# Norm statistics per token in 128x5 blocks, a router fed from raw rows, modulation of gathered rows

## The reference, cut to what is touched

```python
def rms_norm(x, g):
    y = x * lax.rsqrt(jnp.mean(x * x, axis=-1, keepdims=True) + EPS)
    return y * g

def layer_norm(x, g, b):                    # over 512 channels, in the convolution branch
    mu = jnp.mean(x, axis=-1, keepdims=True)
    var = jnp.mean(jnp.square(x - mu), axis=-1, keepdims=True)
    return (x - mu) * lax.rsqrt(var + EPS) * g + b

h = rms_norm(x, lp['rms1_g']) * (1 + sc1) + sh1
...
x = x + g1 * ((ga * y_a + gb * y_b + gc * y_c) @ lp['w_out'])
h2 = rms_norm(x, lp['rms2_g']) * (1 + sc2) + sh2
x = x + g2 * expert_choice_ffn(h2, lp['w_router'], lp['w1'], lp['w3'], lp['w2'])

# expert_choice_ffn, cap = 2 * L // 16: 64 latent and 16 context rows for an expert
aff = jax.nn.softmax(jnp.einsum('bld,de->ble', h, w_router), axis=-1)
gate, idx = lax.top_k(jnp.swapaxes(aff, 1, 2), cap)
xs = jax.vmap(lambda hb, ib: hb[ib])(h, idx)
hid = silu(einsum(xs, w1)) * einsum(xs, w3)
ye = einsum(hid, w2) * gate[..., None]
```

## Time and profile before

| | before |
|---|---|
| time, median of 3 runs | 3113.67 us (3109.89 to 3114.95) |
| profiled execution | 3115.0 us, its span 3113.2 us |
| mean granted clock of TensorE | 0.962 |
| PE busy | 2849.4 us (92%) |
| DVE busy | 1902.1 us (61%) |
| ACT busy | 1502.8 us (48%) |
| DMA read and written | 595.30 MB, mean 191 GB/s |

### The profile page before, as it was taken

One profiled execution on the slowest core, in us unless ns is written; L12 is line 12 of the kernel. 1 busy time (PEld: TensorE's weight loads), 2 busy tenths in 40 slices (PEclk: granted clock), 3 DMA queues, 4 the chain that ended last, 5 costly groups with the idle time before them and its releaser, 6 DMA issues.

```text
span 3113.2 us, 40542 instructions
## 1 busy us (share of the span) xinstructions
PE 2849.4 (92%) x16600; PEld 2226.8 (72%) x16600; DVE 1902.1 (61%) x1901; ACT 1502.8 (48%) x1939; POOL 345.1 (11%) x221
## 2 busy tenths in 40 slices
PE   7999998999996999999779999889999779999996
PEld 6888886888874666666478877778888546666664
DVE  3266556643337888888633666658233488888884
ACT  4244545112226777777532455441122267777773
POOL 0411100000001121111113011100000011111110
PEclk9999998999998999999989999999999889999998
...
GB/s 235 55 102 74 87 89 62 75 68 55 113 204 235 367 376 373 375 375 373 295 53 68 75 102 102 64 63 68 72 55 111 115 283 373 375 374 371 373 375 189
DMA packets 373481, 595.30 MB, mean 191 GB/s; under 512 B 12976, under 2 KB 164656, under 8 KB 373040
## 3 DMA queue, kind: packets, MB, share of 16 engines
...
...
## 4 chain that ended last, share of the span: by engine, by line
PE 68%; DMA 14%; DVE 8%; ACT 5%; issue 3%; SPq 1%; POOL 0%; DVEq 0%; POOLq 0%; ACTq 0%
PE ps L1188 17%; PE ps L1190 16%; PE ps L1189 16%; DMA m_raw<-in_w 11%; PE ps L1425 9%; PE ps L1350 2%; DVE m_lo L1125 2%; PE ps L1383 2%; DMA raw<-in_w_ada 1%; PE ps L1234 1%; ACT probs L513 1%; PE ps L1263 1%; DVE stats L971 1%; PE ps L1372 1%; DMA raw<-in_w_in 1%
## 5 line engine op out<-in xcount | busy, mean ns | idle before, releaser
L779 ACT CAST m_hi<-m_raw 128x2048 fp32r<-128x2048 f32 x384 | 732.9, 1911 | 319.5 <-DMA m_raw<-in_w 271.4
L1125 DVE TENSOR_TENSOR m_lo<-m_raw,m_hi 128x2048 fp32r<-128x2048 f32 x384 | 861.3, 2284 | 16.6 <-PE ps L1190 9.9
L1188 PE MATMUL ps<-h_hi,w_hi 128*128 128x320 f32 (+2 forms) x1408 | 444.6, 316 | 38.1 <-DVE h_lo L896 19.6
L1189 PE MATMUL ps<-h_lo,w_hi 128*128 128x320 f32 (+2 forms) x1408 | 438.7, 312 | 0.0
L1190 PE MATMUL ps<-h_hi,w_lo 128*128 128x320 f32 (+2 forms) x1408 | 438.7, 312 | 0.0
L1188 PE MATMUL ps<-m_hi,xs_hi 128*80 128x512 f32 x1024 | 405.8, 396 | 8.6 <-DVE xs_lo L1142 8.6
L1190 PE MATMUL ps<-m_hi,xs_lo 128*80 128x512 f32 x1024 | 403.3, 394 | 0.0
L1189 PE MATMUL ps<-m_lo,xs_hi 128*80 128x512 f32 x1024 | 403.3, 394 | 0.0
L851 DVE TENSOR_TENSOR w_lo<-raw,w_hi 128x2048 fp32r<-128x2048 f32 x68 | 157.9, 2322 | 303.8 <-ACT w_hi L556 293.5
L556 ACT CAST w_hi<-raw 128x2048 fp32r<-128x2048 f32 x46 | 87.5, 1904 | 528.7 <-DMA raw<-in_w_gate 354.1
L1188 PEld LDWEIGHTS ps<-h_hi,w_hi 128*128 128x128 f32 x1408 | 269.3, 191 | 44.1 <-issue 43.6
...
## 6 DMA issues: line engine op xcount, KB each, us to landing
m_raw<-in_w SPq DMA_DIRECT2D x384, 1024.0 KB, 10.3
...
```

The costliest lines, as they stand in the source:

```text
L779: nc.scalar.copy(m_hi[:, g % HIS], m_raw[:, g % RAWS]).then_inc(s["m_high"], 1)
L1125: nc.vector.tensor_tensor(m_lo[:, g % LOS], m_raw[:, g % RAWS], m_hi[:, g % HIS].bitcast(F32), ALU.subtract).then_inc(s["msplit"], 1)
L1188: pe.matmul(out, wh, xh, start=first, stop=False, skip_group_check=True)
L1189: pe.matmul(out, wh, xl, start=False, stop=False, skip_group_check=True)
```

## The change

All norm statistics are made per token instead of for every partition. A block of 128 tokens becomes the stationary operand and one column of ones the moving one, so that the sums of five blocks stand in five PSUM columns, 128x5 (`square_sums`): 40 matmuls of one column instead of 16 of 320, and 20 instead of 8 for each of the two LayerNorm sums. Root and reciprocal work on 128x5 (`row_scale`). Where the features need them as rows, `spread` multiplies each column, broadcast to 128x128, with the identity (5 matmuls of 128 columns) into PSUM, and DVE reads its factors from there. In norm 1 `spread` stands right behind the sums on PE, in layer 0 ahead of `ada_ahead`; in the merge it stands behind the first branch product of steps 6 and 7 and waits for the statistics.

Norm 2 isn't applied to all rows. The router gets raw x: its columns are scaled by `coef` once (`rv`, two DVE operations), its shift is made by 16 matmuls behind output chunk 0 (`rt_bias`, with a modulation column broadcast as the stationary block and 16 moving columns). `row_stats(c)` makes ten square sums of one column and ten logits products of 16 columns for the two feature chunks of output chunk c; it stands behind output chunk c+1, and the last one at the end. DVE scales the logits by the tokens' factor and adds the shift. The norm's multiplications, its sixteen modulations, the copy `cum` and its transposes go. `h_rows` gets x times the tokens' factor (ACT), and `coef` and shift are applied to the gathered rows of each expert, after their transposes (`rows_modulated`: two DVE operations on 128x640, with the factors laid out for the slots once in a layer by `slot_modulation`, four copies behind L1118). For that `turn_rows` moves from n=9 to n=8, `rows_high` from n=9 to n=10, `rows_low` from n=10 to n=11. ACT's first casts wait for `h_rows` instead of `routed`. The next layer's modulation products move behind the transposes to rows. The output projection cuts its columns 384 and 256 instead of 320 and 320, and the last transposes have three PSUM buffers instead of four. The diff, cut (ACT, DVE and PE in the order of the file):

```diff
+                act.wait_ge(s["r_ready"], seen("r_ready", 2))
                 for t in range(TT):
                     act.wait_ge(s["h2tok_ps"], seen("h2tok_ps"))
                     b = 2 * (t % 2)
-                    nc.scalar.copy(t_all[:, t], flat[:, b * 512:b * 512 + D]).then_inc(s["h2tok"], 1)
+                    nc.scalar.mul(t_all[:, t], flat[:, b * 512:b * 512 + D], st[:, 28 + t:29 + t]).then_inc(s["h2tok"], 1)
...
-                act.wait_ge(s["routed"], seen("routed"))
+                act.wait_ge(s["h2_out"], seen("h2_out", 16 * TT))
...
+            def row_scale():
+                dve.wait_ge(s["ss"], seen("ss"))
+                nc.vector.tensor_scalar(st[:, 28:33], ps[:, 6, 0:TT], 1.0 / D, EPS, ALU.mult, ALU.add).then_inc(s["row_a"], 1)
+                dve.wait_ge(s["row_b"], seen("row_b"))
+                nc.vector.reciprocal(st[:, 28:33], st[:, 28:33]).then_inc(s["r_ready"], 1)
+                dve.wait_ge(s["r_ready"], seen("r_ready"))
...
+                row_scale()
+                dve.wait_ge(s["r_spread"], seen("r_spread"))
                 for k in range(KT):
-                    nc.vector.tensor_tensor(mm_[:, k], x[:, k], row[:], ALU.mult).then_inc(s["tnorm"], 1)
+                    nc.vector.tensor_tensor(mm_[:, k], x[:, k], flat[:, 6 * 512:6 * 512 + TOK], ALU.mult).then_inc(s["tnorm"], 1)
...
+                coefficients(l, 32, "rms2")
+                router = small_at("router").rearrange("p (k e) -> p k e", e=EXPERTS)
+                dve.wait_ge(s["mods_ready"], 2 * l + 2)
+                for c in range(2):
+                    ins = nc.vector.tensor_tensor(rv[:, :, c, :], router, coef[:, :, c:c + 1].to_broadcast([P, KT, EXPERTS]), ALU.mult)
+                ins.then_inc(s["rt_w"], 1)
...
-                coefficients(l, 32, "rms2")
-                norm()
+                row_scale()
 
                 dve.wait_ge(s["logits"], seen("logits"))
-                nc.vector.tensor_copy(cum[:].rearrange("p (a n) -> p a n", a=2), ps[0:EXPERTS, 4:6, 0:HALF]).then_inc(s["logits_out"], 1)
-                dve.wait_ge(s["logits_t"], seen("logits_t"))
                 lg = ps[:, 7, 0:TT * EXPERTS].rearrange("p (t e) -> p t e", e=EXPERTS)
-                link(nc.vector.tensor_reduce(st[:, 8:13], lg, AX.X, ALU.max))
-                nc.vector.tensor_tensor(aff[:], lg, st[:, 8:13].unsqueeze(2).to_broadcast([P, TT, EXPERTS]), ALU.subtract).then_inc(s["rt_a"], 1)
+                link(nc.vector.tensor_tensor(aff[:], lg, st[:, 28:33].unsqueeze(2).to_broadcast([P, TT, EXPERTS]), ALU.mult))
+                nc.vector.tensor_tensor(aff[:, 0:4], aff[:, 0:4], rb[:, 1:2, :].to_broadcast([P, 4, EXPERTS]), ALU.add)
+                link(nc.vector.tensor_tensor(aff[:, 4], aff[:, 4], rb[:, 0], ALU.add))
+                link(nc.vector.tensor_reduce(st[:, 8:13], aff[:], AX.X, ALU.max))
...
+                def slot_modulation():
+
+                    for tile, of in ((coef_t, coef), (shift_t, mods_of[l][:, 24:24 + KT])):
+                        nc.vector.tensor_copy(tile[:, :, 0:CAP_LAT], of[:, :, 1:2].to_broadcast([P, KT, CAP_LAT]))
+                        ins = nc.vector.tensor_copy(tile[:, :, CAP_LAT:], of[:, :, 0:1].to_broadcast([P, KT, CAP_CTX]))
+                    link(ins)
+
+                def rows_modulated():
+
+                    dve.wait_ge(s["xs_ps"], seen("xs_ps"))
+                    link(nc.vector.tensor_tensor(xsm[:], ps[:, 2:4, :].rearrange("p b (k n) -> p (b k) n", k=4)[:, :, 0:SLOTS], coef_t[:], ALU.mult))
+                    nc.vector.tensor_tensor(xsm[:], xsm[:], shift_t[:], ALU.add).then_inc(s["xs_mod"], 1)
...
                     low(g)
+                    if g == 0:
+                        rows_modulated()
                 rows_low()
...
                             turned_low(1)
-                        if n == 10 and e < EXPERTS - 1:
+                            if e < EXPERTS - 1:
+                                rows_modulated()
+                        if n == 11 and e < EXPERTS - 1:
...
+            def square_sums(k0, k1):
+
+                for k in range(k0, k1):
+                    pe.wait_ge(s["sq"], seen("sq"))
+                    for t in range(TT):
+                        ins = pe.matmul(ps[:, 6, t:t + 1], mm_[:, k, t * P:(t + 1) * P], ones[:, 0:1], start=((k, t) == (0, 0)),
+                                        stop=(k == KT - 1), skip_group_check=True)
+                return ins
+
+            def spread(t_sem, t_count, sem):
+
+                pe.wait_ge(s[t_sem], t_count)
+                for t in range(TT):
+                    ins = pe.matmul(flat[:, 6 * 512 + t * P:6 * 512 + (t + 1) * P], st[:, 28 + t:29 + t].to_broadcast([P, P]), ident[:], start=True, stop=True)
+                ins.then_inc(s[sem], 1)
...
-                sum_squares(KT, "sq")
+                square_sums(0, KT).then_inc(s["ss"], 1)
+                spread("r_ready", 2 * l + 1, "r_spread")
                 if l == 0:
-                    ada_ahead((4, 5, 6, 7), (ada_in_a, ada_in_b))
-                    ada_turned(0, 2)
+                    ada_ahead((2, 3, 4, 5), (ada_in_a, ada_in_b))
...
-                            pe.matmul(ps[:, 6, :], ones[:], zc[:, j, 0:LAT], start=(j == 0), stop=(j == GROUPS - 1), skip_group_check=True)
-                            ins = pe.matmul(ps[:, 7, 0:CTX], ones[:], zc[:, j, LAT + CPAD:CRUN], start=(j == 0), stop=(j == GROUPS - 1), skip_group_check=True)
+                            for t in range(TT):
+                                at = t * P if t < 4 else LAT + CPAD
+                                ins = pe.matmul(ps[:, 6, t:t + 1], zc[:, j, at:at + P], ones[:, 0:1], start=((j, t) == (0, 0)),
+                                                stop=(j == GROUPS - 1), skip_group_check=True)
...
+                        if i in (LN_MEAN, LN_VAR) and n == 0:
+                            spread("ln_stat", seen("ln_stat"), "ln_spread")
...
+                def row_stats(c):
+
+                    pe.wait_ge(s["xo_done"], seen("xo_done"))
+                    ins = square_sums(2 * c, 2 * c + 2)
+                    if c == 3:
+                        ins.then_inc(s["ss"], 1)
+                    if c == 0:
+                        pe.wait_ge(s["rt_w"], seen("rt_w", 0))
+                    for k in (2 * c, 2 * c + 1):
+                        for t in range(TT):
+                            ins = pe.matmul(ps[:, 7, t * EXPERTS:(t + 1) * EXPERTS], x[:, k, t * P:(t + 1) * P], rv[:, k, 1 if t < 4 else 0, :],
+                                            start=((k, t) == (0, 0)), stop=(k == KT - 1), skip_group_check=True)
+                    if c == 3:
+                        ins.then_inc(s["logits"], 1)
...
                     if c == 0:
-                        feature_by_k(u, u, "mg_low")
+                        pe.wait_ge(s["rt_w"], seen("rt_w"))
+                        for n in range(2):
+                            for k in range(KT):
+                                ins = pe.matmul(ps[:, 6, (n + 1) * EXPERTS:(n + 2) * EXPERTS], mods_of[l][:, 24 + k, n:n + 1].to_broadcast([P, P]),
+                                                small_at("router")[:, k * EXPERTS:(k + 1) * EXPERTS], start=((n, k) == (0, 0)), stop=(k == KT - 1),
+                                                skip_group_check=True)
+                        ins.then_inc(s["rt_bias"], 1)
                     else:
-                        feature_split(u, u, halves)
+                        row_stats(c - 1)
...
+                pe.wait_ge(s["h2tok"], seen("h2tok", 2))
                 if l < DEPTH - 1:
+                    ada_ahead((4, 7, 2, 3), (ada_in_a, ada_in_c))
                     ada_turned(l + 1, 4)
...
-                        if n == 9 and e < EXPERTS - 1:
-                            turn_rows()
+                            if e < EXPERTS - 1:
+                                turn_rows()
```

160 lines of the change are left out of this document (77 added, 83 removed).

## The result

The changed kernel takes 3155.36 us, median of 4 runs (3154.69 to 3156.08). The kernel before took 3113.14 beside it. The ratio is 1.0137 with a 95% interval of 1.0119 to 1.0154: 42 us slower. The forecast was 3149.9, range 3120 to 3172. The profiled execution took 3156.08 us, span 3154.3, 41.1 over the span of before.

What follows compares the result with a forecast made beforehand. TensorE was taken as the bound outside the experts, the weight stream inside them. Terms 8.7+13.9+2.6+0.6+6.0+1.0+3.4 = +36.2 us on the median of 3113.67 gave 3149.9 us, range 3120 to 3172.

Steps and rivals of the forecast that it cites:

- (1): Start of layer 0: slower square sums, then statistics and spread ahead of the modulation products, +8.7 us.
- (2): Four LayerNorm sums: twenty sparse matmuls each plus spread instead of dense sums, +3.5 us each, +13.9 in all.
- second rival: Clock falls only in streams of 40 in a row, bursts of 16 or 20 keep it: 3130 us, chance 0.09.
- (3): Output projection to first MAX8: added PE matmuls against a shorter tail, +2.6 us in layer 0, +0.6 in layer 1.
- E: End of the last output-projection product; the forecast put the first MAX8 at E+19.5 us.
- (4): Top-k to the first expert product: a longer DVE sequence up to xs_lo, +3.0 us in each layer.
- (5): Steady experts: DVE's chain 1.2 us late at a border, delay paid once, +1 us for both layers.
- third rival: PE stalls at every expert because DVE's 7.4 us chain doesn't move forward: about 3190 us, chance 0.08.
- (6): Layer 0 to layer 1: slower sums, shorter statistics and spread, slower products behind, +3.4 us.
- (7): Next layer's modulation moved behind the token transposes, and three PSUM buffers instead of four: put at nothing.
- first rival: The clock holds in sparse streams, making the kernel faster: 3103 us, chance 0.11.
- attention (0): Projections and attention, up to the first gate cast: no change forecast, 0 us.

Runs made afterwards that it cites:

- experiment 6: Changed kernel with norm 1 and LayerNorm sums 128 columns wide, row sums and logits 96 wide, xs_hi and xs_lo casts one step earlier: 3111.31 us.
- experiment 1: Changed kernel with 128 moving columns of ones instead of one in the sums of norm 1 and the LayerNorm: 3140.81 us.
- experiment 2: Changed kernel with the cast of xs_hi at n=9 instead of 10 and xs_lo at n=10 instead of 11: 3146.97 us.
- 8: Kernel before with two extra DVE operations per expert at n=9 and xs_lo at n=11 instead of n=10: 3130.33 us.
- 5: Kernel before with two extra DVE operations per expert at n=9, written to an unread tile, xs_lo unmoved: 3116.95 us.
- 4: Kernel before with two extra DVE operations per expert at n=2, written to an unread tile: 3115.82 us.
- (9): Kernel before with two extra DVE operations per expert at n=9 and the gathered rows turned at n=8 instead of n=9: 3127.34 us.

## Why the prediction was right, and where it was not

The time and the direction held, and the mechanism given for the direction is there: the clock falls in or behind the streams of few columns. Between the traces of the changed kernel and of experiment 6 (40 us), the four stretches whose sums were widened (start, merge, output projection, layer 0 to 1) make up 35 us and the experts 17; attention and top-k went 12 the other way. But that the sum came within 6 us is luck. One term was too small by 25.7 us, one too large by 11, and 10 us in attention, put at nothing, are chance as far as the traces go. The largest term of the measured sum, the experts, is one that the prediction put at 1. It would have made the kernel slower with the clock held too: the 3111 us of experiment 6 and its 17 us less in the experts give some 3128, an estimate.

(1) *Start of layer 0*, +8.7: measured 9.1. The forty sums cost 16.04 us, not 14.5. From the start of the sums the first product is 10.1 us later than before in the changed kernel and 0.9 in experiment 1: all but about 1 us is the clock.

(2) *LayerNorm*, +3.5 each: measured 7.6 a layer, 3.8 each. The split was another one. In layer 0 the sums kept their clock nearly to their end (4.9 and 4.4 us instead of 5.9), and the dense products behind them lost it (3.0 and 1.8 us, against experiment 1, instead of the 0.8 put there). These bursts are paid for mostly after they have ended. The test named in the prediction, a clock of 0.50 over the LayerNorm sums and over the row sums between the output chunks, would have gone against it: the mean is 0.90 and 1.00 over layer 0's LayerNorm sums, and over the row sums and logits between the chunks it is 0.71 at 890.17 and 1.00 at 911.94. By that sign it was the second rival, in which bursts keep their clock; but its +5.2 for both layers, against 15.2 measured, left out the products behind them.

(3) *Output projection and top-k*, +2.6 and +0.6: measured −1.4 and −6.8. MAX8 came at E+17.0 in both layers, not E+19.5: the row sums and logits of chunk 2 ran wholly at the full clock (4.4, not 5.9), and so did a part of those of chunk 3. The additions between the chunks came to 16.9 and 13.5 us, not 18.4. The step that failed is the fall put at 3.0 us after the start of every burst: it came in the changed kernel between 1 and 5 us after it. Nor is E+17.0 fixed. Experiment 1 has these forty matmuls as they are, and there the fall came 2.3 us behind E, with MAX8 at E+20.2 in both layers:

```profile
917.86 2.29 PE L1307 MATMUL ps<-ones,m 128*128 128x1 f32 x20
920.01 4.29 PE L1558 MATMUL ps<-router_scaled,x 128*128 128x16 f32 x20
924.14 4.41 PE L1307 MATMUL ps<-ones,m 128*128 128x1 f32 x20
928.40 4.43 PE L1558 MATMUL ps<-router_scaled,x 128*128 128x16 f32 x20
```

(4) +3.0 a layer: measured 2.5. The copies for the slots took 1.0 us, not 2.1; DVE waited 2.6 us for the turned rows, about as reckoned.

(5) *Steady experts*, "the delay is paid once", +1: measured 26.7. This step failed. The arithmetic was right: 7.4 us of chain, 1.2 us late. Wrong was the sentence that the weights would then be ahead and the chain start earlier. These are ACT's waits for weights and SP's for a free raw slot in 13 experts, in the kernel before (1044 to 1504) and, in the second block, in the changed kernel (1055 to 1528):

```profile
ACT m_hi L779 <- DMA m_raw<-in_w: 122.9, 141, 2.5
SPq L125 <- DVE m_lo L1125: 381.1, 155, 6.2
```

```profile
ACT m_hi L786 <- DMA m_raw<-in_w: 130.7, 130, 4.5
SPq L125 <- DVE m_lo L1150: 396.9, 156, 6.7
```

ACT waits for weights as long as before (122.9 and 130.7 us), though PE is late, and SP issues a weight DMA only when DVE's split has freed a raw slot (155 and 156 waits). As I read these rows, what makes PE late makes the splits late, and these the DMAs, so that a delay at a border is handed round and the weights don't get ahead; no run with more slots tests this. That PE waits at nearly every border is the third rival, to which the prediction gave 0.08, at a smaller price: the chain's part is 14 us (experiment 2) to 17 (8 over 5) instead of 36 to 45. Experiments 2 and 8 show the chain from both sides, 4 and 5 that the DVE time as such is worth 2 to 3 us a layer. The last 3 us a layer may be PE's earlier turn (9), which isn't shown.

(6) +3.4: measured 3.2. (7) At nothing: PE was done with the modulation 5.4 us before top-k's end, as hoped.

The first rival, in which the clock holds in sparse streams (3103 us), falls by the window at 22.40: 14.50 us at half clock in a PE that is busy 14.50 us. The Trainium skill in "TensorE: Matmul & The Clock Gate", section "Why this matters for your kernels", names idle gaps of PE for such drops; that window goes against them as the only cause.

The forecast of attention (0) had no row against it, but also none that showed how far one execution stands for others. A stretch at half clock from a 2 us wait on is in one trace and not in the next.
